# Two mixture layers: the first four weight units are multiplied ahead of TensorE's branch, and VectorE copies the first turn's tokens

## The reference

```python
def hierarchical_moe(h, wr_g, br_g, wr_e, br_e, w_gate, w_up, w_down):
    p_g = jax.nn.softmax(xf @ wr_g + br_g)         # 4 groups, the best one is taken
    ...
    top_v, top_i = lax.top_k(sel, TOP_K_IN_GROUP)  # 2 of its 8 experts
    gate = w_g[:, None] * jax.nn.softmax(top_v, axis=-1)
    ...
    return (jax.nn.silu(xb @ w_gate[e]) * (xb @ w_up[e])) @ w_down[e]   # for each expert
    ...
    out = zeros.at[row_tok].add(y * row_w[:, None])
```

## Time and profile before

| | us |
|---|---|
| median of 3 runs | 2001.03 |
| lowest and highest | 1999.12, 2011.39 |
| the profiled execution | 2006.36 |
| its span | 2004.5 |

### The profile page before, as it was taken

The page is one execution under the profiler, slowest core; times in us unless marked ns, Lnnn a source line. Parts: engine busy times, 40 slices in busy tenths (PEclk is TensorE's granted clock), DMA queues, the critical chain, the costliest instruction groups (busy, mean ns, idle before and its releaser), DMA issues. The chain is left out here.

```text
span 2004.5 us, 29934 instructions
## 1 busy us (share of the span) xinstructions
PE 1783.8 (89%) x12646; PEld 1318.7 (66%) x12646; DVE 1085.9 (54%) x1973; ACT 644.9 (32%) x1013; POOL 10.5 (1%) x6
## 2 busy tenths in 40 slices
PE   6888789888887899989996999999998988769998
PEld 5332266573322588878875788878886877557887
DVE  4332243353322577742378586677666564558665
ACT  3111012241110444422233554455443502136443
POOL 0000000000000000000000000000000000100000
PEclk9898889788988899999997899999999989679999
DMA  9899971358999955513420355535542412044540
GB/s 362 368 420 421 421 280 36 132 196 360 422 420 421 384 181 184 182 59 114 181 84 1 126 210 187 188 129 195 187 167 95 147 41 87 4 147 168 189 168 22
DMA packets 58189, 405.26 MB, mean 202 GB/s; under 512 B 6416, under 2 KB 7824, under 8 KB 10432
## 3 DMA queue, kind: packets, MB, share of 16 engines
q1 hardware_dynamic: 58048, 403.25, 52.4%
HBM read 402.18 MB, written 1.05 MB: 201 GB/s over the span
## 5 line engine op out<-in xcount | busy, mean ns | idle before, releaser
L1995 PE MATMUL ps<-ffn_x,ffn_wh 128*128 128x512 f32 x1408 | 497.1, 407 | 9.9 <-DVE ffn_x L2129 7.1
L1998 PE MATMUL ps<-ffn_x,ffn_wl 128*128 128x256 f32 x1408 | 376.7, 281 | 0.0
L1995 PEld LDWEIGHTS ps<-ffn_x,ffn_wh 128*128 128x128 f32 x1408 | 270.1, 192 | 84.2 <-issue 11.0
L2136 DVE TENSOR_TENSOR ffn_wl<-w,ffn_wh 128x2048 fp32r<-128x2048 f32 x132 | 301.6, 2287 | 1.6
L1998 PEld LDWEIGHTS ps<-ffn_x,ffn_wl 128*128 128x128 f32 x1408 | 258.2, 189 | 1.6
L2080 ACT CAST ffn_wh<-w 128x2048 fp32r<-128x2048 f32 (+1 forms) x140 | 252.7, 1805 | 6.3 <-PEq L711 5.2
L2095 ACT COPY ffn_part_low<-ps 128x512 f32<-128x512 f32 x88 | 51.5, 586 | 339.0 <-PE ps L1998 338.7
L2140 DVE TENSOR_TENSOR ffn_z<-ps,ffn_part_low 128x512 f32<-128x512 f32 x88 | 60.8, 691 | 161.5 <-ACT ffn_part_low L2095 161.3
L2039 PE MATMUL ps<-ffn_wh,ffn_hidh 128*128 128x512 f32 x352 | 138.3, 393 | 0.4 <-issue 0.4
L2041 PE MATMUL ps<-ffn_wh,ffn_hidl 128*128 128x512 f32 x352 | 137.5, 391 | 0.0
L2040 PE MATMUL ps<-ffn_wl,ffn_hidh 128*128 128x512 f32 x352 | 137.3, 390 | 0.0
(11 more groups left out here) (537 smaller groups left out, 2709.1 us busy)
## 6 DMA issues: line engine op xcount, KB each, us to landing
w<-in_ffn_gu SPq DMA_DIRECT2D x88, 1024.0 KB, 4.8
w<-in_moe_gu SPq DMA_DIRECT2D x70, 1024.0 KB, 22.9
w_extra<-in_moe_gu SPq DMA_DIRECT2D x52, 1024.0 KB, 26.5
w<-in_ffn_dn SPq DMA_DIRECT2D x44, 1024.0 KB, 4.8
w_extra<-in_moe_dn SPq DMA_DIRECT2D x32, 1024.0 KB, 26.3
w<-in_moe_dn SPq DMA_DIRECT2D x26, 1024.0 KB, 26.8
sq<-in_moe_dn SPq DMA_DIRECT2D x6, 1024.0 KB, 28.0
sq<-in_moe_gu SPq DMA_DIRECT2D x6, 1024.0 KB, 27.9
```

What stands on the lines that cost most here:

```text
L1995: return nc.tensor.matmul(pair_of(b)[:, a], high[:, s, tile(a, k)], X[:, k], start=k == 0, stop=False)
L1998: return nc.tensor.matmul(pair_of(b)[:, a, 0:SEQ], low[:, s, tile(a, k)], XH[:, k], start=False, stop=k == KT - 1)
L2136: nc.vector.tensor_tensor(low[:, s], S.buf(units[n]), high[:, s], ALU.subtract).then_inc(*w_split.one())
```

## The change

- PE, ahead of the branch: the second half's gather is split around the first half's transposes; after it come units 0 and 1, the second half's transposes, and units 2 and 3. They raise no semaphore.
- PE, after the branch: unit 4 comes first and raises `gu_done` by 5, then the gather of turn 1, and the rest in the old order.
- DVE makes all four copies of turn 0 and `choose(1)` within `route`'s vector part, ahead of its branch; the last copy comes after the gates are computed. ACT's part ahead of the branch falls away. Copies of later turns stay where they were; semaphore counts are shifted to match.
- `experts_over_all` gets four small matmuls that close the open accumulation (not run with these inputs).

The diff, cut to its core:

```diff
             act.wait_ge(*counted.at(1))
             fullest = K.fullest(act, count)
-            in_slots["scalar_first"](act)
             with act.If(fullest > CAP):
...
-            routing["vector"](dve, in_slots["vector_first"])
...
         dve.wait_ge(*placed.at(1))
-        build_first(dve, 0)
+        choose_first(dve, 0)
         dve.wait_ge(*x_taken.at(2))
         low(1)
+        copy_first(dve)
+        choose_first(dve, 1)
+        copy_second(dve)
         dve.wait_ge(*exd.at(2))
...
         v.tensor_tensor(groups(gate[:]), in_group(32), of_group, ALU.mult).then_inc(*priced.one())
         dve.wait_ge(*priced.now())
+        copy_last(dve)
...
+        def gather(i, half, parts=(0, 1, 2)):
+
+            if 0 in parts:
...
+            f, to = slice(half * 512, (half + 1) * 512), K.ps[:, 2 + half, :]
+            for t in parts:
+                if t < 2:
+                    nc.tensor.matmul(to, sel[:, i % 2, t], xh[:, t, f], start=t == 0, stop=False)
+                    nc.tensor.matmul(to, sel[:, i % 2, t], xl[:, t, f], start=False, stop=False)
+                else:
+                    nc.tensor.matmul(to, selr[:, i % 2], xr[:, f], start=False, stop=True).then_inc(x_made.sem, 1)
...
+                pe.wait_ge(xs_v.sem, half + 1)
+            elif half == 0:
+                pe.wait_ge(xs_a.sem, i)
             else:
-                pe.wait_ge(xs_a.sem, 2)
+                pe.wait_ge(xs_v.sem, i + 2)
...
-        def gate_up(i, ks):
+        def gate_up(i, ks, ahead=False):
...
                                           start=k == 0, stop=k == KT - 1, tile_position=(0, j * CAP))
-                mm.then_inc(gu_done.sem, 1)
+                if not ahead:
+                    mm.then_inc(gu_done.sem, 5 if i == 0 and k == 4 else 1)
...
         if first:
             gather(0, 0)
-            gather(0, 1)
+            gather(0, 1, (0,))
             turn_x(0, 0)
+            gather(0, 1, (1, 2))
+            pe.wait_ge(xg_v.sem, 1)
+            gate_up(0, (0, 1), ahead=True)
             turn_x(0, 1)
+            gate_up(0, (2, 3), ahead=True)
             return
-        pe.wait_ge(xg_a.sem, 1)
-        gate_up(0, (0, 1, 2, 3))
+        pe.wait_ge(xg_v.sem, 2)
+        gate_up(0, (4,))
         gather(1, 0)
         gather(1, 1)
-        gate_up(0, (4,))
         turn_x(1, 0)
         gate_up(0, (5,))
         turn_x(1, 1)
...
 
-        if first:
-            take_slots(0, 0)
-            take_slots(0, 1)
-            take_x(0, 0)
-            take_x(0, 1)
-            return
...
+        def take_slots(i, half=1):
+            dve.wait_ge(x_made.sem, 4 * i + 1 + half if i else 2 * half + 1)
+            v.tensor_copy(xs[:, half], K.ps[:, 2 + half]).then_inc(xs_v.sem, 1)
+
+        def take_x(i, half=1):
+            dve.wait_ge(x_made.sem, 4 * i + 3 + half if i else 2 * half + 2)
+            v.tensor_copy(xg[:, i % 2, 4 * half:4 * half + 4], K.ps[:, 2 + half].rearrange("p (k s) -> p k s", k=4)).then_inc(xg_v.sem, 1)
...
-            if i + 1 < TURNS:
+            if i and i + 1 < TURNS:
                 choose(i + 1)
...
@@ -1220,6 +1236,8 @@
     def tensor(pe):
         pe.wait_ge(*priced.at(1))
         pe.wait_ge(first_taken.sem, 2)
+        for j in range(4):
+            nc.tensor.matmul(K.ps[j * CAP:(j + 1) * CAP, 0, 0:L1], K.con(C_ONE, CAP), K.xn[:, 0], start=False, stop=True, tile_position=(0, j * CAP))
         for i, (t0, tn) in enumerate(Q_TILES_1):
             nc.tensor.matmul(K.ps[:, 6, t0:t0 + tn], small[0:tn, i, 21:22].to_broadcast([tn, P]), K.cst[0:tn, C_ID:C_ID + tn], start=True, stop=True)
         for i, (t0, tn) in enumerate(Q_TILES_1):

```

More of the change, by code:

```diff
@@ L765, in _ @@
         def _(dve):
-            routing["vector"](dve, in_slots["vector_first"])
+            routing["vector"](dve, in_slots["choose_first"], in_slots["copy_first"], in_slots["copy_second"], in_slots["copy_last"])
             dve.wait_ge(*counted.at(1))
@@ L869, in scalar, with vector @@
         nc.scalar.activation(small[:, :, 57:58], small[:, :, 56:57], ACT.Exp).then_inc(*exd.one())
-    def vector(dve, build_first):
+    def vector(dve, choose_first, copy_first, copy_second, copy_last):
         def do(ins):
@@ L971, in tensor, with turn_x @@
     def tensor(pe, first=False):
[L972 to L981, removed]
-            if i == 0:
[L983 to L996, removed]
+        def gather(i, half, parts=(0, 1, 2)):
+            if 0 in parts:
+                if half == 0:
+                    pe.wait_ge(sel_made.sem, i + 1)
+                    if i >= 2:
+                        pe.wait_ge(hidT_made.sem, i - 1)
+                elif i >= 2:
+                    pe.wait_ge(spread_taken.sem, i - 1)
+                if i == 0:
+                    pe.wait_ge(*x_taken.at(half + 1))
+                    pe.wait_ge(*xl_made.at(half + 1))
+            f, to = slice(half * 512, (half + 1) * 512), K.ps[:, 2 + half, :]
[5 more added lines that the diff above has]
+                    nc.tensor.matmul(to, selr[:, i % 2], xr[:, f], start=False, stop=True).then_inc(x_made.sem, 1)
+        def turn_x(i, half):
+            if i == 0:
+                pe.wait_ge(xs_v.sem, half + 1)
+            elif half == 0:
+                pe.wait_ge(xs_a.sem, i)
             else:
-                pe.wait_ge(xs_a.sem, 2)
+                pe.wait_ge(xs_v.sem, i + 2)
             for k in range(4):
@@ L1003, in turn_gates @@
         def turn_gates(i):
-            pe.wait_ge(xg_v.sem, min(i + 1, TURNS - 1))
+            pe.wait_ge(xg_v.sem, min(i + 1, TURNS - 1) + 2)
             onehot = [(sel[:, i % 2, t] if t < 2 else selr[0:N_META, i % 2]).bitcast(F32) for t in range(3)]
@@ L1073, in tensor @@
         for i in range(1, TURNS):
-            pe.wait_ge(xg_a.sem, i + 2)
+            pe.wait_ge(xg_a.sem, i)
             gate_up(i, (0, 1))
@@ L1082, in tensor @@
                 by_token(i - 1, range(4, KT))
-                pe.wait_ge(xg_v.sem, i)
+                pe.wait_ge(xg_v.sem, i + 2)
                 gate_up(i, (4, 5, 6, 7))
@@ L1101, in tensor, with scalar @@
         by_token(TURNS - 1, range(4, KT))
-    def scalar(act, first=False):
+    def scalar(act):
         def take_slots(i, half):
@@ L1135, in scalar, with vector @@
                 nc.scalar.copy(spread[:, i % 2], K.ps[:, 3, 0:L1]).then_inc(spread_taken.sem, 1)
-    def vector(dve, first=0):
+    def vector(dve, first=""):
         v = nc.vector
@@ L1173, in split_y @@
             v.tensor_tensor(yt[:, 1, at], K.ps[:, 4 + half], yt[:, 0, at], ALU.subtract).then_inc(y_split.sem, 1)
-        if first:
+        if first == "choose 0":
             choose(0)
+            return
+        if first == "choose 1":
+            choose(1)
+            return
+        if first == "copy first":
+            take_slots(0, 0)
+            return
+        if first == "copy second":
+            take_x(0, 0)
+            take_slots(0, 1)
+            return
+        if first == "copy last":
+            take_x(0, 1)
             return
@@ L1198, in experts_in_slots @@
     return {"tensor": tensor, "scalar": scalar, "vector": vector, "tensor_first": lambda pe: tensor(pe, True),
-            "scalar_first": lambda act: scalar(act, True), "vector_first": lambda dve, i: vector(dve, 1),
-            "room": (xg, xs), "first_taken": xg_a}
+            "choose_first": lambda dve, i: vector(dve, "choose 1" if i else "choose 0"), "copy_first": lambda dve: vector(dve, "copy first"),
+            "copy_second": lambda dve: vector(dve, "copy second"), "copy_last": lambda dve: vector(dve, "copy last"),
+            "room": (xg, xs), "first_taken": xg_v}
 def experts_over_all(K, layer, ctx, small, room, first_taken, gate, priced, gu, dn, gu_done, dn_done):
```

## The result

The changed kernel is slower by a little: the median of 22 runs is 2012.38 us against 2004.53 us for 22 runs of the kernel before beside it. The measured ratio is 1.0043 with a 95% interval of 1.0034 to 1.0052 (the two medians alone would give 1.0039). That is 8.6 us (6.8 to 10.4) on 2001.03 us, within 1%, and outside my range of 1995.5 to 2005.5. The profiled execution took 2008.29 us (span 2006.4, granted clock 0.919; before 2006.36, 2004.5, 0.919). The two profiled executions are thus only 1.9 us apart: the traces show where the kernels differ, but not the whole 8.6 us.

A forecast was written before the change was run, and what follows sets the result against it. The weight stream, restarted by SP's first issue, was taken to bound both layers. Terms -0.75 - 0.25 (layer 0) and +0.4 - 0.7 (layer 1) gave -1.3 us on 2001.03: 1999.7, range 1995.5 to 2005.5.

The forecast's parts named there:

- What bounds the layers: Both mixture layers: a layer ends when its weight stream ends, a fixed number of bytes after restart at some 422 GB/s.
- The order and its times ahead of the branch: PE before L748: units 0 to 3 run ahead, branch reached at 58.8 and 461.2, sequencer about 37 instructions ahead.
- Rival A: PE's sequencer takes the branch only near unit 3's end (60.5, 462.9): +3.0 us, 2004.0; chance 0.2.
- The branch's price: PE's wait at L748 for its instruction fetch: 3.3 us per layer, between 2.4 and 4.07.
- first matmul 0.17 after the branch, second half 0.43 later: Unit 4 behind the branch frees the units 1.23 us after it; SP issues at 63.4 and 465.7.
- The clock at the fifth product: Unit 4 after the branch: a fallen clock would make its halves slower, 0.9 us more; not in the sum.
- Five units at once: SP's five issues in a row: stream as if full 1.5 us after the issue, giving back 0.25 and 0.7 us.
- VectorE's and ScalarE's parts at nothing: VectorE's added copies and later branch, and ScalarE's four lost copies, hold nobody: 0 us.

The follow-up runs named there:

- changed_shifted: Changed kernel plus eight never-run matmuls on layer 1's side not taken, moving the branch target by 32 instructions; 1.0033 of the kernel before (+6.6 us).
- the swapped pair: Kernel before and changed kernel, each with TensorE's two branch sides exchanged, slots' side directly behind the branch; 1.0009 and 1.0044 of the kernel before.
- copies_only: Kernel before with only VectorE's four copies and early slot choice moved ahead of its branch, all products behind PE's branch; 1.0007 (+1.4 us).
- changed_again: The changed kernel run once more with no edit; 1.005 of the kernel before (+10 us).
- before_shifted: Kernel before plus 23 never-run matmuls (92 instruction places) on layer 1's side not taken; 1.0015 of the kernel before (+3.0 us).
- early_free: changed_shifted with the release of the four ahead units put on unit 4's first group; in the trace still at the unit's end; 1.0025 (+5.0 us).

## Why the prediction was wrong, point by point

**What bounds the layers** held. A late stream start stayed late to the layer's end in layer 1, and taking PE's stop away gave 9 us in two kernels.

**The order and its times ahead of the branch** held in layer 0: L748 at 58.9 for 58.8. The time was right in part by luck. PE began unit 0 at 56.43 where I had 56.8, and when the branch was reached, eight of the 32 instructions of units 2 and 3 had started: the sequencer was 24 ahead by my count, not 37. The two errors cancel. In layer 1 it came at 460.7 for 461.2, but the gather had started 1.5 us earlier (451.4 for 452.9), so relative to the layer it was 0.9 late; the row of units 0 and 1 is 2.38 us long where it is 1.92 in layer 0, the clock being low for part of it. Rival A, a branch at the end of unit 3, did not happen.

**The branch's price** was a term mis-sized: 3.3 us taken, 4.3 and 3.85 measured (3.4 to 4.5 in the other changed kernels with nothing freed early). The 3.3 us were 2.4 from the packet's start to going on and 0.9 before it. Layer 1 took 2.3 and 1.5. Layer 0 took 3.3 and 1.0; another instruction packet had started at 59.0, just before the branch's at 59.9, but no run shows whether that is the cause. In layer 0 this 1.0 us is the whole miss: SP's first issue at 64.47 for 63.4.

**The step that failed** is "first matmul 0.17 after the branch, second half 0.43 later". In layer 1 PE went on at 464.5, exactly as forecast by the clock of the run (counted from the layer's first gather product it was 1.5 us late, which the layer's earlier start hides), but the second half started at 468.03, not 465.1 (+2.9), and took 1.9 us at the lower clock where I had 0.6 to SP (+1.3). Together that is the 4.3 us between 465.7 and 469.98. I had counted one fetch for a branch. There are two when the target stands just before a block's end. The trace of the kernel before shows the second packet, 0.8 us behind the end of each branch, at 62.8 and 463.9; it cannot show where the changed kernel's target would lie. The change moves code on both sides of the branch, and I priced no bound for that. This step is not the whole miss: changed_shifted, without the second stop, still has +6.6 us where the forecast was -1.3.

**The clock at the fifth product** I had named ("0.9 more") and left out of the sum. The low clock came in three of four profiles in layer 0, and in layer 1 in the first. The stop itself precedes it: all four unit-4 rows of layer 0 follow 2.6 to 2.7 us without a product.

**Five units at once** held as far as the ramp goes: by the table's stretches the stream behaves as if full 1.5 us after the issue in both layers (66.0 less 64.5, 471.4 less 470.0), as read from the burst at 436.23. That holding four units back costs by itself is what the swapped pair shows.

**VectorE's and ScalarE's parts at nothing** is not contradicted, but copies_only leaves up to 4.6 us open.

**Where the 8.6 us are.** The stream starts of the two layers together are 5.5 us later in the first profile and 5.3 us in changed_again; the block's end in layer 1 is 3.0 to 4.2 us of it, the joint release with its longer fetch and low clock the rest. Some 3 us stay open, and 4 to 5 in changed_again and changed_shifted (10 us measured for 5.3 of stream, 6.6 for 2.4), so the stream starts account for a third to two thirds of the loss. Two observations bear on the rest. In changed_again layer 0 takes 210.1 us from stream start to the end of its last product (by_token's), in the first profile and before 207.0 and 207.3; its last down product runs at the lower clock:

```profile
268.95 1.94 PE L1047 MATMUL ps<-w,slot_hidT 128*32 128x512 f32 x8 [1.33 <-DMA w<-in_moe_dn]
```

But layer 0 of before_shifted takes 210.6 us too, so this is not shown to belong to the change. And the mean granted clock over the 22 runs is 0.9169, against 0.9199, 0.9194 and 0.9187 in three other sets of runs of before; runs with a lower clock tend to be longer. Side by side it is 0.9181 for 0.9199 in changed_again but 0.9198 for 0.9194 in early_free, so a lower clock does not come with the change every time. What sets it was not tested, and the cause of these last microseconds stays open.

## What to carry to other kernels

A taken branch cost its engine an instruction fetch here, and if the engine's next products are what frees buffers, price it as part of the transfer chain: in these runs about 4 us into idle DMA, 6 to 7 us behind a full weight stream. Moving work ahead of it helps only what does not need to be released; if the releases stay behind, the stop and the low clock after it fall on the one product that everything waits for. When an edit changes the amount of code near a branch, look at where the target falls: a block's end 10 to 15 instructions behind it was a second stop.

Check in the trace that a semaphore moved in the source also moved in time, since one matmul of the program can be several products.

## What I had not expected of the hardware

- A second fetch after a branch's target: 1.7 to 2.2 us idle after four products, at the same product in changed and changed_again, gone with 32 unexecuted instructions more, and made in the kernel before with 92 (1.3 us idle there). Where the weights' queue was dry, the packet of the following block starts 0.7 to 1.2 us after PE goes on from the branch.
- The length of a branch depends on the DMA load: 3.4 to 4.9 us where the weights' queue was dry or nearly so (5.3 in layer 0 of before, reached while it still ran), 5.9 and 6.0 at a layer's end and 6.5 and 7.1 at its start with it full.
- After 2.6 us without a product, the clock was sometimes high for the next one (1.07 us for eight products) and sometimes low (1.9 us), with the same program.
